# Reordering the first mixer of block 2: compression weights ahead of the later queries, more column steps between turning and weighting, and other places for the weight splits

## The chip, the cores and the metric

The kernel runs on one core of a Trainium2 chip. The metric is the device time of one execution in microseconds, median of several executions. Lower is better.

## The reference, cut to what matters

The network has two blocks of two layers over 256 tokens of width 1024. The change touches one mixer, the first of block 2 (nsa_mixer, called the compressed-and-selected attention below). All in float32:

```
proj = h @ w_in
q, kc_t, vc_t, ks, vs, kw, vw, gate = split(proj)     # q: 16 heads of 64; the rest 4 groups of 64
q, kc_t, ks, kw = rope(...)
kcmp = silu(windows(kc_t) @ cmp_w1[0]) @ cmp_w2[0]     # 15 windows of 32 tokens, 2048 -> 256 -> 64
vcmp = silu(windows(vc_t) @ cmp_w1[1]) @ cmp_w2[1]
p_cmp = softmax(q . kcmp);  o_cmp = p_cmp @ vcmp
o_slc = selected attention(q, ks, vs)                  # at 256 tokens every block is selected
o_win = banded attention(q, kw, vw)
return (g0 * o_cmp + g1 * o_slc + g2 * o_win) @ w_out
```

## The kernel before, in words

**Weights.** Every weight matrix is streamed from memory in units of 128 x 2048 floats (1 MB each), in the order in which they are used. A unit passes four stations. The SyncE queue loads it into one of three buffers `raw` (unit u goes to buffer u mod 3; its load is issued when VectorE has done with unit u-3, which stood there before). ScalarE copies it to `w_hi`, rounded to the short form that TensorE multiplies at full speed (`split_to` in the scalar program, line 1113). VectorE takes the difference `w_lo` (`split_to` in the vector program, line 1527) and sets `lo_done`, which both lets TensorE use the unit and frees its `raw` buffer. `w_hi` and `w_lo` have six places. TensorE multiplies every tile three times (`three`, lines 347, 350 and 351: high by high, high by low, low by high).

**One order per engine.** No scheduler is at work. Each engine runs its instructions in the order in which the code writes them, and waits on semaphores where the code says so. `split_to(n)` splits the units up to n-1 at that place of the engine's order; if a unit has not been loaded yet, the engine stands there, with everything that is written behind it.

**The mixer** is stage `nsa`. Its first unit is u0; below, "unit i" is u0+i. Units 0 to 5 are the first projections, unit 6 the selected values, units 7 and 8 the compression weights of the keys (`compress_weights(.., kv=0)`, 16 column steps of three products each), unit 9 the window values, and then, before the change, unit 10 (queries 1), units 11 and 12 (compression weights of the values), unit 13 (queries 2) and unit 14 (queries 3). Units 15 to 18 are the output projection.

The attention is cut into 20 jobs (`nsa_job`). For each job n, TensorE multiplies `scores(n)` (lines 883 to 887); VectorE takes `maxima(n)` (1926, 1927); ScalarE `exponentials(n)` (1379, 1381); VectorE `weights(n)` (1949, 1950, 1953); GpSimd multiplies the second token tile (`second_tile_weights`, line 2191); TensorE turns the result (`transposed(n)`, 901 to 903; 897 for a compressed job); ScalarE and VectorE copy it out of PSUM (`copy_turned(n)`, lines 1391 and 1958); TensorE multiplies it by the values (`weighted(n)`, 921, 922). "Turning" is `transposed`, "weighting" is `weighted`, and the two copies between them are a hand-over. TensorE fills the time of these chains with column steps of the weight units: the dictionaries in calls such as `unit(10, 6, {1: lambda: transposed(2), ...})` say ahead of which step a piece of the attention stands. A step of `unit` or `values` is two times three products, a step of `compress_weights` three.

The compressed keys and values take their own way: `hidden_exp` and `hidden` (lines 1401; 1974 to 1976) form the silu of a compression, `turn_hidden` (936) turns it, `compress` (944, 948) multiplies by the second matrix. The queries pass `take` (1570, 1571), `times_cos` on GpSimd (2182), `rot` on TensorE (839) and `rope` (1894, 1896).

Of the kernel before, what the change touches and what calls it, by code (L numbers as in the profile page):

```python
# [25 lines left out]
NWIN = GROUPS * NCMP  # L26
# [97 lines left out]
def network_kernel(nc, stream, x_in, consts_in, cols_in, p_in, count_in, table_in, out):  # L124
# [12 lines left out]
    with ctx:  # L137
# [201 lines left out]
        def _(pe):  # L339
# [444 lines left out]
            def nsa(s, u0):  # L784
# [192 lines left out]
                def last_of_first(n):  # L977
                    pe.wait_ge(nsa_v.sem, 2)
                    weighted(n)
# [23 lines left out]
                compress_weights(7, 5, 0, {6: lambda: transposed(0), 10: lambda: (weighted(0), scores(2))})  # L1003
                values(9, 4, {0: lambda: transposed(1), 2: lambda: (weighted(1), scores(3))})
                pe.wait_ge(nsa_v.sem, 1)
                unit(10, 6, {1: lambda: transposed(2), 3: lambda: weighted(2), 5: lambda: transposed(3), 7: lambda: weighted(3)})
                pe.wait_ge(hidc_ready.sem, 1)
                compress_weights(11, 5, 1, {4: lambda: rot(5, 6)})
                pe.wait_ge(nsa_v.sem, 2)
                unit(13, 4, {4: turn_hidden})  # L1010
                pe.wait_ge(rope_done.sem, 5)
                unit(14, 6, {0: compress, 2: lambda: rot(6, 4), 5: lambda: scores(4), 6: lambda: scores(5)})
                rot(7, 6)
                for n in (4, 5):
                    transposed(n)
                    pe.wait_ge(*tA_done.due(me))
                    scores(n + 2)
                weighted_cmp(0, 0)
# [9 lines left out]
                for n in (14, 15):  # L1028
                    transposed(n)
                    pe.wait_ge(*tA_done.due(me))  # L1030
                    scores(n + 2)
# [67 lines left out]
        def _(act):  # L1099
# [251 lines left out]
            def nsa(s, u0):  # L1351
# [47 lines left out]
                def hidden_exp(kv):  # L1399
                    act.wait_ge(unit_used.sem, u0 + 9 + 4 * kv)  # L1400
# [24 lines left out]
                split_to(u0 + 10)  # L1425
                values(0, u0 + 7, 6)
                split_to(u0 + 11)
                copy_turned(0)
                split_to(u0 + 12)
                exponentials(2)  # L1430
                copy_turned(1)
                hidden_exp(0)
                exponentials(3)
                act.wait_ge(unit_used.sem, u0 + 9)
                nc.scalar.activation(hid_hi[:, 0:NWIN * 16], at(NSA_WIN + 16 * NWIN, NWIN * 16), ACT.Copy).then_inc(win_hi.sem, 1)
                values(1, u0 + 10, 4)
                split_to(u0 + 13)
                copy_turned(2)
                split_to(u0 + 14)
                copy_turned(3)  # L1440
                split_to(u0 + 16)
                hidden_exp(1)
                hidden_keys()
# [5 lines left out]
                exponentials(6)  # L1449
                exponentials(7)  # L1450
                heads_high(0)
                for n in range(6, NSA_JOBS):
# [7 lines left out]
                    if n in (7, 8):  # L1460
                        split_to(u0 + 12 + n)
# [966 lines left out]
```

## Time and profile before

| | before |
|---|---|
| median of 3 executions | 1750.73 us (1748.95 to 1754.86) |
| profiled execution, its own time | 1749.38 us |
| its span, first to last instruction | 1747.6 us |
| mean granted TensorE clock | 0.988 of 2.4 GHz |
| TensorE busy | 1677.4 us, 96% of the span |

The span is the time from the first to the last instruction of the profiled execution; the 1.8 us beside it are start and end. TensorE is the engine that is hardly ever idle, so the time goes down only where TensorE waits less, and up where it waits more. The mixer lies between 1013 us and 1228 us of the span.

### The profile page before, as it was taken

Reading aid. Unit: us, or ns where it says so; the run is one execution under the profiler, and the core shown is the slowest. Engines: PE = TensorE matmul, PEld = TensorE weight load, DVE = VectorE, ACT = ScalarE, POOL = GpSimd, SP = SyncE. Lnnn points to the kernel's source line nnn. Section 1 sums busy time; section 2 is a strip of 40 time slices with the busy share of each in tenths; the row PEclk is TensorE's granted clock in tenths of the full one; section 3 lists DMA queues with packets and bytes.
Section 4 is the critical chain, followed back from the end, with each engine's and each line's share of the span. In section 5 each row is a group of like instructions: output and inputs, shape, how many; then the busy total and the mean of one; then the engine's idle time right before and its main releaser. Section 6 shows DMA issues by size and latency. Waiting matters only on the chain.

```text
span 1747.6 us, 29361 instructions
## 1 busy us (share of the span) xinstructions
PE 1677.4 (96%) x12278; PEld 1570.9 (90%) x12278; DVE 1072.3 (61%) x1072; ACT 799.5 (46%) x950; POOL 146.7 (8%) x113
## 2 busy tenths in 40 slices
PE   7999999899999999999999999888899999999998
PEld 7999986799999999989999998756899989888997
DVE  7554776375557755577555687644765567556563
ACT  5343558253435533355434555243544465444442
POOL 1000123010001100012000131121000001000000
PEclk9999999999999999999999999898999999999999
DMA  7545451155453554555453443310365534335551
GB/s 295 201 152 208 159 180 72 73 199 212 150 215 146 193 195 166 200 197 187 157 215 147 161 186 128 130 56 25 123 211 177 188 145 184 108 119 185 179 189 48
DMA packets 39633, 282.27 MB, mean 162 GB/s; under 512 B 4417, under 2 KB 4545, under 8 KB 5761
## 3 DMA queue, kind: packets, MB, share of 16 engines
q1 hardware_dynamic: 39168, 279.59, 43.3%
q8 instruction: 63, 1.03, 0.2%
q0 software_dynamic: 384, 1.51, 0.2%
q14 instruction: 18, 0.14, 0.0%
HBM read 280.04 MB, written 1.05 MB: 161 GB/s over the span
## 4 chain that ended last, share of the span: by engine, by line
PE 87%; DVE 5%; ACT 4%; issue 1%; DMA 1%; POOL 1%; POOLq 0%; DVEq 0%; SPq 0%; ACTq 0%
PE ps L347 27%; PE ps L350 27%; PE ps L351 27%; DVE w_lo L1527 1%; DMA raw<-weights 1%; ACT w_hi L1113 1%; PE ps L883 1%; ACT arena L1381 0%; POOL arena L2191 0%; PE ps L876 0%; DVE arena L1763 0%; ACT arena L1379 0%; DVE X L1668 0%; PE ps L747 0%; PE ps L921 0%
## 5 line engine op out<-in xcount | busy, mean ns | idle before, releaser
L347 PE MATMUL ps<-hT_hi,w_hi 128*128 128x256 f32 x2392 | 683.7, 286 | 15.1 <-DVE hT_lo L1539 12.3
L350 PE MATMUL ps<-hT_lo,w_hi 128*128 128x256 f32 x2392 | 678.2, 284 | 0.0
L351 PE MATMUL ps<-hT_hi,w_lo 128*128 128x256 f32 x2392 | 678.1, 283 | 0.0
L1527 DVE TENSOR_TENSOR w_lo<-raw,w_hi 128x2048 fp32r<-128x2048 f32 x264 | 600.4, 2296 | 124.6 <-ACT w_hi L1113 124.6
L1113 ACT ACTIVATE w_hi<-raw 128x2048 fp32r<-128x2048 f32 x264 | 495.8, 1904 | 40.0 <-DMA raw<-weights 39.9
L347 PEld LDWEIGHTS ps<-hT_hi,w_hi 128*128 128x128 f32 x2392 | 460.1, 192 | 19.2 <-DVE w_lo L1527 11.4
L350 PEld LDWEIGHTS ps<-hT_lo,w_hi 128*128 128x128 f32 x2392 | 460.4, 192 | 2.1 <-issue 1.0
L351 PEld LDWEIGHTS ps<-hT_hi,w_lo 128*128 128x128 f32 x2392 | 460.2, 192 | 0.0
L350 PE MATMUL ps<-hid_lo,w_hi 128*128 128x256 f32 x744 | 211.3, 284 | 0.0
L347 PE MATMUL ps<-hid_hi,w_hi 128*128 128x256 f32 x744 | 210.6, 283 | 0.0
L351 PE MATMUL ps<-hid_hi,w_lo 128*128 128x256 f32 x744 | 208.4, 280 | 0.0
L1154 ACT ACTIVATE sil<-sil 128x512 f32<-128x512 f32 x44 | 27.8, 632 | 345.3 <-DVE sil L1570 345.2
L1570 DVE TENSOR_TENSOR sil<-ps,spare 128x512 f32<-128x512 f32 x47 | 32.5, 691 | 221.0 <-PE ps L351 220.8
L351 PEld LDWEIGHTS ps<-hid_hi,w_lo 128*128 128x128 f32 x744 | 142.9, 192 | 0.0
L350 PEld LDWEIGHTS ps<-hid_lo,w_hi 128*128 128x128 f32 x744 | 142.9, 192 | 0.0
L347 PEld LDWEIGHTS ps<-hid_hi,w_hi 128*128 128x128 f32 x744 | 139.9, 188 | 0.0
L347 PE MATMUL ps<-w_hi,hid_hi 128*128 128x512 f32 (+1 forms) x296 | 114.1, 386 | 4.2 <-DVE hid_lo L1627 3.3
L350 PE MATMUL ps<-w_lo,hid_hi 128*128 128x512 f32 (+1 forms) x296 | 113.9, 385 | 0.0
L351 PE MATMUL ps<-w_hi,hid_lo 128*128 128x512 f32 (+1 forms) x296 | 112.0, 378 | 0.0
L2163 POOL TENSOR_TENSOR arena<-arena 128x512 f32<-128x512 f32 x27 | 40.3, 1491 | 822.5 <-ACT arena L1133 465.0
L347 PE MATMUL ps<-w_hi,hT_hi 128*128 128x512 f32 (+1 forms) x280 | 102.9, 368 | 2.7 <-DVE hT_lo L1962 2.6
L350 PE MATMUL ps<-w_lo,hT_hi 128*128 128x512 f32 (+1 forms) x280 | 99.1, 354 | 0.0
(273 smaller groups left out, 1736.0 us busy)
## 6 DMA issues: line engine op xcount, KB each, us to landing
raw<-weights SPq DMA_DIRECT2D x264, 1024.0 KB, 4.8
X<-x SPq DMA_DIRECT2D x2, 512.0 KB, 6.8
out<-X SPq DMA_DIRECT2D x4, 256.0 KB, 2.1
arena<-p POOLq DMA_DIRECT2D x2, 256.0 KB, 5.3
arena<-counts POOLq DMA_DIRECT2D x1, 512.0 KB, 5.7
arena<-nsa_tables POOLq DMA_DIRECT2D x1, 448.0 KB, 6.8
const<-constants SPq DMA_DIRECT2D x1, 427.0 KB, 9.7
cols<-parameters SPq DMA_DIRECT2D x1, 213.5 KB, 2.5
```

The source lines that it names most:

```text
L347: mm = nc.tensor.matmul(dst, a_hi, b_hi, start=start, stop=False, skip_group_check=True)
L350: nc.tensor.matmul(dst, a_hi, b_lo, start=False, stop=False, skip_group_check=True)
L351: return nc.tensor.matmul(dst, a_lo, b_hi, start=False, stop=stop, skip_group_check=True)
L883: nc.tensor.matmul(bank(a, r * 256, 256), q_of(h, P), k_of(br, h, 256), start=r == 0, stop=False, skip_group_check=True)
L1113: nc.scalar.activation(unit_cols(w_hi, u, 0, UNIT), raw[:, r * UNIT:(r + 1) * UNIT], ACT.Copy).then_inc(hi_done.sem, 1)
L1154: nc.scalar.activation(sil[:, 0:512], sil[:, 0:512], ACT.Silu).then_inc(silu_done.sem, 1)
L1527: nc.vector.tensor_tensor(unit_cols(w_lo, u, 0, UNIT), raw[:, r * UNIT:(r + 1) * UNIT], f(unit_cols(w_hi, u, 0, UNIT)), ALU.subtract).then ...
L1570: return nc.vector.tensor_tensor(chunked(dst), chunked(src), by_token(2), ALU.mult)
L2163: step(nc.gpsimd.tensor_tensor(total, total, at(SQUARES + b * 512, 512), ALU.add))
```

## The change

Four things are done in this one stage; no instruction is added or removed.

1. Units 10 and 11 are now the compression weights of the values, and unit 12 is queries 1. TensorE runs `compress_weights(10, 5, 1, ...)` ahead of `unit(12, ...)`.
2. The steps between `transposed(n)` and `weighted(n)` grow: for job 0 from 4 to 8 compression steps, for jobs 1 to 3 likewise, and jobs 4 to 7 are spread over the steps of unit 14.
3. In ScalarE's order the splits stand in other places relative to `values`, `copy_turned` and `exponentials`.
4. In VectorE's order `maxima`, `weights`, `low_windows`, `hidden`, `take` and the splits are interleaved anew, and the splits that stood between jobs 7 and 9 (on both engines) stand ahead of the steady loop.

```diff
@@ -974,9 +974,10 @@
...
-    def last_of_first(n):
-        pe.wait_ge(nsa_v.sem, 2)
-        weighted(n)
+    def next_scores(n):
+        pe.wait_ge(*tA_done.due(me))
+        scores(n)
...
@@ -1000,22 +1001,20 @@
...
     pe.wait_ge(dup_act.sem, 4)
-    compress_weights(7, 5, 0, {6: lambda: transposed(0), 10: lambda: (weighted(0), scores(2))})
-    values(9, 4, {0: lambda: transposed(1), 2: lambda: (weighted(1), scores(3))})
+    compress_weights(7, 5, 0, {5: lambda: transposed(0), 13: lambda: (weighted(0), scores(2))})
+    values(9, 4, {0: lambda: transposed(1), 4: lambda: (weighted(1), scores(3))})
+    pe.wait_ge(hidc_ready.sem, 1)
+    compress_weights(10, 5, 1, {3: lambda: transposed(2), 10: lambda: weighted(2), 12: lambda: transposed(3)})
     pe.wait_ge(nsa_v.sem, 1)
-    unit(10, 6, {1: lambda: transposed(2), 3: lambda: weighted(2), 5: lambda: transposed(3), 7: lambda: weighted(3)})
-    pe.wait_ge(hidc_ready.sem, 1)
-    compress_weights(11, 5, 1, {4: lambda: rot(5, 6)})
+    unit(12, 6, {2: lambda: weighted(3), 6: turn_hidden})
     pe.wait_ge(nsa_v.sem, 2)
-    unit(13, 4, {4: turn_hidden})
+    unit(13, 4, {1: lambda: rot(5, 6), 4: compress})
     pe.wait_ge(rope_done.sem, 5)
-    unit(14, 6, {0: compress, 2: lambda: rot(6, 4), 5: lambda: scores(4), 6: lambda: scores(5)})
+    unit(14, 6, {0: lambda: scores(4), 1: lambda: scores(5), 2: lambda: rot(6, 4), 5: lambda: transposed(4), 6: lambda: next_scores(6),
+                 7: lambda: transposed(5)})
+    next_scores(7)
+    weighted_cmp(0, 0)
     rot(7, 6)
-    for n in (4, 5):
-        transposed(n)
-        pe.wait_ge(*tA_done.due(me))
-        scores(n + 2)
-    weighted_cmp(0, 0)
     steady(6, ((0, 0), (0, 1)))
...
@@ -1027,8 +1026,7 @@
...
         transposed(n)
-        pe.wait_ge(*tA_done.due(me))
-        scores(n + 2)
+        next_scores(n + 2)
     weighted_cmp(2, 0)
...
@@ -1397,7 +1395,7 @@
...
     def hidden_exp(kv):
-        act.wait_ge(unit_used.sem, u0 + 9 + 4 * kv)
+        act.wait_ge(unit_used.sem, u0 + 9 + 3 * kv)
         nc.scalar.activation(HIDC[0:NWIN, kv * CMP_HID:(kv + 1) * CMP_HID], bank(5, 0, CMP_HID)[0:NWIN], ACT.Exp, scale=-1.0).then_inc(hid_exp.sem, 1)
...
@@ -1422,24 +1420,24 @@
...
     exponentials(1)
-    split_to(u0 + 10)
+    split_to(u0 + 12)
     values(0, u0 + 7, 6)
-    split_to(u0 + 11)
+    split_to(u0 + 13)
     copy_turned(0)
-    split_to(u0 + 12)
+    split_to(u0 + 14)
+    act.wait_ge(unit_used.sem, u0 + 9)
+    nc.scalar.activation(hid_hi[:, 0:NWIN * 16], at(NSA_WIN + 16 * NWIN, NWIN * 16), ACT.Copy).then_inc(win_hi.sem, 1)
     exponentials(2)
...
     hidden_exp(0)
+    split_to(u0 + 15)
     exponentials(3)
-    act.wait_ge(unit_used.sem, u0 + 9)
-    nc.scalar.activation(hid_hi[:, 0:NWIN * 16], at(NSA_WIN + 16 * NWIN, NWIN * 16), ACT.Copy).then_inc(win_hi.sem, 1)
     values(1, u0 + 10, 4)
-    split_to(u0 + 13)
     copy_turned(2)
-    split_to(u0 + 14)
+    split_to(u0 + 16)
     copy_turned(3)
-    split_to(u0 + 16)
     hidden_exp(1)
+    split_to(u0 + 17)
     hidden_keys()
...
@@ -1447,8 +1445,9 @@
...
     exponentials(6)
+    heads_high(0)
     exponentials(7)
-    heads_high(0)
+    split_to(u0 + 19)
     for n in range(6, NSA_JOBS):
...
@@ -1457,8 +1456,6 @@
...
             heads_high({9: 1, 15: 2, 19: 3}[n])
-        if n in (7, 8):
-            split_to(u0 + 12 + n)
     split_to(u0 + 21)
...
@@ -2013,54 +2010,55 @@
...
     nc.vector.tensor_copy(at(GATES, 96), bank(6, 256, 96)).then_inc(gates_ready.sem, 1)
+    maxima(0)
     dve.wait_ge(rope_done.sem, 2)
     take(u0 + 6, 7, QS[1])
-    maxima(0)
     maxima(1)
+    weights(0)
     low_windows(0)
     split_to(u0 + 9)
+    weights(1)
     rope(4, 7, at(KT + 512, 512))
-    weights(0)
-    weights(1)
     split_to(u0 + 10)
...
     copy_turned(1)
-    split_to(u0 + 12)
+    low_windows(1)
     weights(2)
     hidden(0)
+    split_to(u0 + 12)
     maxima(3)
-    low_windows(1)
     copy_turned(2)
...
     copy_turned(3)
-    dve.wait_ge(rope_done.sem, 3)
-    take(u0 + 11, 6, QS[0], QSCALE)
     split_to(u0 + 14)
-    rope(5, 6, at(QT + 512, 512))
-    split_to(u0 + 16)
     hidden(1)
     hidden_values()
+    dve.wait_ge(rope_done.sem, 3)
+    take(u0 + 13, 6, QS[0], QSCALE)
+    split_to(u0 + 15)
+    rope(5, 6, at(QT + 512, 512))
+    compressed()
+    split_to(u0 + 16)
+    maxima(4)
+    maxima(5)
     dve.wait_ge(rope_done.sem, 4)
     take(u0 + 14, 4, QS[1], QSCALE)
-    compressed()
+    weights(4)
+    weights(5)
     rope(6, 4, at(QT + 1024, 512))
     split_to(u0 + 17)
-    maxima(4)
-    maxima(5)
+    t_full.due(me, 2)
+    maxima(6)
     dve.wait_ge(rope_done.sem, 5)
     take(u0 + 15, 6, QS[0], QSCALE)
-    weights(4)
-    weights(5)
+    maxima(7)
+    heads_low(0)
+    weights(6)
     rope(7, 6, at(QT + 1536, 512))
-    split_to(u0 + 18)
-    t_full.due(me, 2)
-    maxima(6)
-    maxima(7)
-    weights(6)
-    heads_low(0)
+    split_to(u0 + 19)
     for n in range(6, NSA_JOBS):
...
@@ -2069,8 +2067,6 @@
...
             heads_low({9: 1, 15: 2, 19: 3}[n])
-        if n in (7, 8):
-            split_to(u0 + 12 + n)
     split_to(u0 + 21)
...
@@ -2397,7 +2393,7 @@
...
     w1 = v["nsa_cmp_w1_2"][0]
-    for part in (kc, vc, ks, qs[0], gates, kw, vs, w1[0], vw, qs[1], w1[1], qs[2], qs[3]):
+    for part in (kc, vc, ks, qs[0], gates, kw, vs, w1[0], vw, w1[1], qs[1], qs[2], qs[3]):
         units += as_units(chunks(part))
...
```

`next_scores(n)` is the wait for `copy_turned` on ScalarE and then `scores(n)`.

The following rows show the built programs. First ScalarE of the kernel before, from the exponentials of job 1 (line 1381) to the copy of job 1 (the second row of line 1391). Line 1113 is the split of a unit, 1367 takes the selected values, 1391 is `copy_turned`.

```order
L1381 ACTIVATE arena,stat<-ps,stat 128x256 x2
L1113 ACTIVATE w_hi<-raw 128x2048
L1367 ACTIVATE arena<-ps,stat 128x256 x2
L1113 ACTIVATE w_hi<-raw 128x2048
L1391 ACTIVATE arena<-ps 128x512
L1113 ACTIVATE w_hi<-raw 128x2048
L1379 ACTIVATE arena,stat<-ps,stat 128x128 x2
L1381 ACTIVATE arena,stat<-ps,stat 128x256 x2
L1391 ACTIVATE arena<-ps 128x512
```

The same place of the changed kernel, where the lines of these helpers have lower numbers (1111, 1365, 1389, 1377 and 1379), and, after the mark, the piece from the split ahead of job 3's exponentials to the copy of job 3.

```order
L1379 ACTIVATE arena,stat<-ps,stat 128x256 x2
L1111 ACTIVATE w_hi<-raw 128x2048 x3
L1365 ACTIVATE arena<-ps,stat 128x256 x2
L1111 ACTIVATE w_hi<-raw 128x2048
L1389 ACTIVATE arena<-ps 128x512
...
L1111 ACTIVATE w_hi<-raw 128x2048
L1377 ACTIVATE arena,stat<-ps,stat 128x128 x2
L1379 ACTIVATE arena,stat<-ps,stat 128x256 x2
L1365 ACTIVATE arena<-ps,stat 128x256 x2
L1389 ACTIVATE arena<-ps 128x512
L1111 ACTIVATE w_hi<-raw 128x2048
L1389 ACTIVATE arena<-ps 128x512
```

Ahead of the first copy (job 0) there stood the splits of units 9 and 10; now there stand those of units 9, 10, 11 and 12. The split of unit 14 stands ahead of the exponentials of job 3 and the copy of job 2, and the split of unit 15 ahead of the copy of job 3; before, units 12 and 13 stood at these places (ahead of the copies of jobs 2 and 3).

Next VectorE of the changed kernel, from the copy of job 0 (line 1955, before 1958) to the split that follows job 3's copy. Line 1524 is the split of a unit (before 1527), 1923 a maximum, 1972 and 1973 the end of `hidden(0)`, 1950 the end of `weights(3)`.

```order
L1955 COPY arena<-ps 128x256
L1524 TENSOR_TENSOR w_lo<-raw,w_hi 128x2048
L1923 TENSOR_REDUCE stat<-ps 128x2
...
L1972 RECIPROCAL arena<-arena 60x256
L1973 TENSOR_TENSOR arena<-arena,ps 60x256
L1524 TENSOR_TENSOR w_lo<-raw,w_hi 128x2048
...
L1950 TENSOR_TENSOR arena<-arena,stat 128x256
L1524 TENSOR_TENSOR w_lo<-raw,w_hi 128x2048
L1955 COPY arena<-ps 128x256
L1524 TENSOR_TENSOR w_lo<-raw,w_hi 128x2048
```

The split of unit 11 (the second of these rows of line 1524) has moved behind `hidden(0)`; before, it stood ahead of `weights(2)` and `hidden(0)`. The split of unit 12 (the third) still stands right behind `weights(3)` and ahead of the copy of job 3.

## Rows read from the trace of the kernel before

**Rows 1.** The page: engines over the span, and the chain that ended last.

```profile
PE 1677.4 (96%) x12278; PEld 1570.9 (90%) x12278; DVE 1072.3 (61%) x1072; ACT 799.5 (46%) x950; POOL 146.7 (8%) x113
...
PE 87%; DVE 5%; ACT 4%; issue 1%; DMA 1%; POOL 1%; POOLq 0%; DVEq 0%; SPq 0%; ACTq 0%
```

**Rows 2.** Windows: stretch, its length, each engine's busy time, granted clock, DMA.

```profile
1064.00:1107.40 43.40, 36.23 (x291) 33.01 (x290) 31.76 (x34) 18.99 (x34) 8.04 (x6) 1.00 0.48 180
...
1107.40:1110.80 3.40, 3.40 (x19) 3.40 (x18) 0.52 (x2) 3.37 (x2) 0.00 (x0) 0.50 0.29 120
...
1127.90:1138.10 10.20, 9.13 (x27) 6.45 (x26) 7.03 (x14) 3.22 (x15) 0.41 (x1) 0.50 0.29 103
```

**Rows 3.** Timeline, TensorE at its waits: start, length, instruction, [idle before <-releaser].

```profile
1064.84 0.30 PE L901 MATMUL ps<-const,arena 128*128 128x128 f32 x1 [0.32 <-POOL arena L2191]
...
1068.66 0.66 PE L921 MATMUL ps<-arena 128*64 128x256 f32 x4 [1.54 <-issue]
...
1087.46 0.66 PE L921 MATMUL ps<-arena 128*64 128x256 f32 x4 [2.14 <-ACT arena L1391]
...
1106.29 0.45 PE L936 MATMUL ps<-const,arena 60*128 60x60 f32 x4 [3.16 <-DVE arena L1976]
...
1125.50 1.12 PE L839 MATMUL ps<-sil,arena 128*128 128x512 f32 x2 [0.85 <-DVE sil L1571]
...
1127.53 0.44 PE L897 MATMUL ps<-const,arena 128*128 128x128 f32 x2 [0.90 <-DVE arena L1944]
...
1128.44 1.22 PE L883 MATMUL ps<-arena 64*128 64x256 f32 x2 [0.47 <-ACT arena L1389]
...
1139.12 0.30 PE L901 MATMUL ps<-const,arena 128*128 128x128 f32 x1 [1.14 <-POOL arena L2191]
```

**Rows 4.** Timeline, TensorE: the first products of two following column steps.

```profile
1101.16 0.28 PE L347 MATMUL ps<-hT_hi,w_hi 128*128 128x256 f32 x1
...
1101.53 0.28 PE L347 MATMUL ps<-hT_hi,w_hi 128*128 128x256 f32 x1
```

**Rows 5.** Timeline, ScalarE: units 10, 11, 15; copy of job 0; exponentials of job 3, windows.

```profile
1063.26 1.97 ACT L1113 ACTIVATE w_hi<-raw 128x2048 fp32r<-128x2048 f32 x1
...
1065.72 0.60 ACT L1391 ACTIVATE arena<-ps 128x512 f32<-128x512 f32 x1 [0.49 <-PE ps L903]
...
1066.94 1.91 ACT L1113 ACTIVATE w_hi<-raw 128x2048 fp32r<-128x2048 f32 x1 [0.62 <-DMA raw<-weights]
...
1081.78 0.37 ACT L1379 ACTIVATE arena<-ps,stat 128x128 f32<-128x128 f32 x1 [6.75 <-DVE stat L1927]
...
1083.38 1.01 ACT L1435 ACTIVATE hid_hi<-arena 128x960 fp32r<-128x960 f32 x1
...
1094.76 1.92 ACT L1113 ACTIVATE w_hi<-raw 128x2048 fp32r<-128x2048 f32 x1 [1.72 <-DMA raw<-weights]
```

**Rows 6.** Timeline, VectorE: units 8, 9, 12; copy of job 0; silu, first and last.

```profile
1059.44 2.29 DVE L1527 TENSOR_TENSOR w_lo<-raw,w_hi 128x2048 fp32r<-128x2048 f32 x1
...
1065.10 3.13 DVE L1527 TENSOR_TENSOR w_lo<-raw,w_hi 128x2048 fp32r<-128x2048 f32 x1
...
1068.15 0.41 DVE L1958 COPY arena<-ps 128x256 f32<-128x256 f32 x1
...
1086.95 2.76 DVE L1527 TENSOR_TENSOR w_lo<-raw,w_hi 128x2048 fp32r<-128x2048 f32 x1 [0.28 <-ACT w_hi L1113]
...
1103.73 0.28 DVE L1974 TENSOR_SCALAR arena<-arena 60x256 f32<-60x256 f32 x1
...
1105.82 0.41 DVE L1976 TENSOR_TENSOR arena<-arena,ps 60x256 f32<-60x256 f32 x1
```

**Rows 7.** Timeline, GpSimd: the multiplications of jobs 0 and 1.

```profile
1063.42 2.66 POOL L2191 TENSOR_TENSOR arena<-arena,stat 128x512 f32<-128x512 f32 x2 [5.47 <-DVE stat L1950]
```

**Rows 8.** Timeline, TensorE: waits in the steady loop.

```profile
1153.01 0.66 PE L921 MATMUL ps<-arena 128*64 128x256 f32 x4 [1.35 <-issue]
...
1159.82 0.66 PE L921 MATMUL ps<-arena 128*64 128x256 f32 x4 [2.04 <-issue]
```

## The prediction

> **What bounds the kernel now.** The page first: TensorE is busy for 96% of the span and holds 87% of the chain that ended last [rows 1]. So the time moves only with TensorE's waits and with its clock. The windows come next: in the mixer TensorE is busy for 36.2 us of 43.4 us between 1064.0 and 1107.4 us, and there are stretches at half clock, 3.4 us from 1107.4 and 10.2 us from 1127.9, each behind waits [rows 2]. The timeline of TensorE then gives every wait that the change could touch: 0.32 and 1.54 us ahead of the turning and weighting of job 0, 2.14 us ahead of the weighting of job 2, 3.16 us ahead of `turn_hidden`, 0.85, 0.90 and twice 0.47 us around jobs 4 to 7 (one row stands for two), 1.14 us ahead of the turning of job 6 [rows 3], and in the steady loop among others 1.35 and 2.04 us [rows 8].
>
> Next, who is late. Behind job 0 it is not ScalarE, whose copy starts at 1065.72 us [rows 5], but VectorE's copy, which starts at 1068.15 us: it stands behind a split of 3.13 us [rows 6], lengthened because GpSimd multiplies jobs 0 and 1 from 1063.42 to 1066.08 us [rows 7]. The reader should take from this that a hand-over waits for every split written ahead of it. The other fact is how far splits can run ahead. VectorE ends unit 8 at 1059.44 + 2.29 = 1061.73 us [rows 6], and ScalarE starts unit 11, in the same raw buffer, at 1066.94 us, released by its transfer [rows 5]: 5.2 us. Unit 12 ends at 1086.95 + 2.76 = 1089.71 [rows 6] and unit 15 starts at 1094.76 us [rows 5]: 5.05 us. So **a unit reaches ScalarE 5.1 us after VectorE has split the unit three before it**, and takes 1.9 us there.
>
> **What the change does, wait by wait.** I walk the new orders of all four engines forward with the durations of the rows. A column step of three products takes 0.36 us [rows 4]. All products stay; TensorE's work costs nothing more.
>
> A. *Weighting of job 0.* ScalarE now has units 9 to 12 ahead of this copy, where it had 9 and 10. Unit 12 needs VectorE to be through with unit 9. That ended at 1065.10 + 3.13 = 1068.2 us [rows 6]; in the new order it ends near 1067.3, because GpSimd's multiplications fall earlier. Unit 12 lands at 1067.3 + 5.1 = 1072.4, is split at 1074.3, and the copy (0.6 us [rows 5]) ends at 1074.9. TensorE began the compression at 1064.84 - 0.32 - 6 x 0.36 = 1062.4, and turns job 0 at 1064.2 without a wait. In the old order the turning and four steps took 1068.66 - 1.54 - 1064.84 = 2.3 us [rows 3]; four more steps make 3.7, so it arrives at 1067.9 us. Wait 7.0 us, where there were 0.32 + 1.54: **+5.1**. Behind it on TensorE stand the scores of job 2, on which VectorE and then ScalarE wait; behind the split on ScalarE stand the copies of jobs 0 and 1.
>
> B. *Weighting of job 2.* Unit 14 now stands ahead of the exponentials of job 3, `values(1)` and the copy of job 2. It needs VectorE's unit 11, which has moved behind `hidden(0)`. The weighting and the scores of job 2 take 0.8 + 1.8 us (1068.66 to 1071.3 in the old order [rows 3]), three steps 1.1, so the first compression ends near 1078.6 us; ScalarE's window copy (1.0), exponentials (1.6, the distance of two rows), copy and exponential of the silu end at 1082.1; `hidden(0)` takes 2.5 us (1103.73 to 1106.23 in the second silu), and unit 11 is done at 1082.1 + 2.5 + 2.3 = 1086.9 [rows 5, 6]. Then 5.1 us of transfer, 1.9 of split, 1.6 of exponentials, 0.6 of values and 0.6 of copy: 1096.7 us. TensorE has 16 + 10 steps (9.4 us), two turnings (1.3) and the weighting and scores of jobs 1 and 3 (2.6) behind 1078.6: it arrives at 1091.9. Wait 4.8 for 2.14 [rows 3]: **+2.7**.
>
> C. *Weighting of job 3.* Unit 15 stands ahead of this copy. It needs unit 12 of VectorE, which stands behind `weights(3)`, so behind the late exponentials: it starts at 1096.3 and ends at 1099.8 (2.2 us, and 1.3 us behind GpSimd's multiplication of job 3, as in [rows 6, 7]). Transfer, split and copy end at 1099.8 + 5.1 + 1.9 + 0.6 = 1107.4 us; TensorE arrives at 1101.7. Wait 5.7 where there was none: **+5.7**.
>
> D. *`turn_hidden`.* Between the second compression and it there now lie six double steps of unit 12 and the wait C. Its silu ends about 1110.3 us (exponential behind the copy of job 3, then 2.5 us), TensorE comes at 1112.5: the 3.16 us go [rows 3]: **-3.2**.
>
> E. *Jobs 4 to 7 and the turning of job 6.* Spread over the steps of unit 14, the short waits of job 4 and 5 vanish, and one of 1.3 us stays ahead of `rot(7)`. The rows have 0.85 + 0.90 + 0.47 + 0.47 + 1.14 us [rows 3], but part of this stretch ran at half clock, where products are longer and waits shorter [rows 2]. Walked at full clock, the old order waits 7.0 us here and the new one 3.9 (2.6 of it ahead of job 6): **-3.1**.
>
> F. *Steady loop.* The splits no longer stand between jobs 7 and 9, where waits of 1.35 and 2.04 us were [rows 8]; they stand ahead of the copy of job 6, whose weighting then waits 3.3 us. **-0.7**. Behind job 9 the two orders are the same.
>
> Sum: 5.1 + 2.7 + 5.7 - 3.2 - 3.1 - 0.7 = **+6.5 us**. The edits in the order of the stream cost nothing, since unit 10 stays a load of the same size.
>
> G. *Clock.* At half clock 3.4 us of busy TensorE do the work of 1.7 us. A wait of 3.16 us was followed by such a stretch, waits of 1.54 and 2.14 us were not [rows 2, 3]. Three waits of 5 to 7 us should each be followed by one: at most 3 x 1.7 = +5.1, at least 0 where the next wait takes the loss in (B and C end on chains that TensorE hardly moves), and the old stretch at 1107.4 (-1.7) may go. I take **+2.5**, between -1.7 and +5.1, nearer the upper end since the new waits are longer than the one that was followed by a stretch.
>
> Total +9.0 us. The profiled execution took 1749.4 us (its span plus 1.8), so 1758.4; the median shown is 1.4 us above it, so 1759.8 or, rounded, **1760 us**, 0.5% slower. What a measurement of this kernel tells from no change is about 0.3%, 5.3 us. The walk has its own error: led over the old order it ends 3 us early over 200 us, its waits within 1 us each. Landing 4.8 us (the page's median) instead of 5.1 takes 0.3 us from A, B and C each.
>
> On waiting in order, the Trainium skill (page TensorE: Matmul & The Clock Gate, section "Architectural detail: the array is 16× 32×32, not 1× 128×128") says that ScalarE and VectorE work strictly first in, first out. The trace agrees, with VectorE's copy at 1068.15 us. Without that rule A, B and C would vanish and the sum be about 1742.
>
> **The rivals.**
> *Faster: the hand-overs are not held.* If unit 12 were in its buffer when ScalarE came to it, the longer distances would do their work: A -1.9, B -2.1, C 0, D -3.2, E and F up to -3.8: 1750.7 less 7 to 11, 1740 to 1744 us. It decides at one point: VectorE must end unit 9 before about 1060 us, and the rows have it at 1068.2 [rows 6]. Chance 0.05.
> *No change.* The waits are as long as I say at A, but B and C are chained to VectorE's unit 11: if the silu and the split end 3 us sooner, or transfers land in 4 us, B and C shrink by 2 to 3 us each and the sum is +2 to +5: 1752 to 1755 us. For it speaks that units 13 to 15 have slack in the old order; against it, the two measured landings. Chance 0.08.
> *More half clock.* Every long wait brings a slow stretch, A's is extended by short waits behind it, as from 1127.9 us where three such lengths followed each other [rows 2], and none is absorbed: 6.5 + 7 and more: 1763 to 1767 us. Chance 0.12, inside "slower".
> The Trainium skill (page TensorE: Matmul & The Clock Gate, section "What's actually happening") calls half rate the default that only activity releases. By that rule alone G would be near +5 and the time 1762 us; the waits of 1.54 and 2.14 us without a stretch behind them speak for less.
> *My forecast:* slower by 5.3 to 12 us, chance 0.75.
>
> **Numbers.** Faster 0.05, same 0.08, slower 0.87 (0.75 + 0.12). The range 1754 to 1767 us takes in the upper half of "no change" and the clock's bound, and leaves the faster case out.
>
> **What would show it.** Right: TensorE's rows of line 921 with waits of about 7, 5 and 6 us, released by ScalarE's copy; ScalarE's split ahead of each released by the transfer; no wait ahead of the transposes of `turn_hidden`; half-clock stretches behind the long waits. Wrong: ScalarE's units 11 and 12 splitting without waiting for a transfer, or the long waits released by VectorE. The prediction fails most likely in E and F, where I compare two chains of many links, and in G.

## The result

The changed kernel takes 1764.34 us (median of 7 runs, 1760.37 to 1766.91), the kernel before 1750.73 us (now of 7 runs, 1748.70 to 1757.70): ratio 1.0068, 95% interval 1.0049 to 1.0087. That is 0.7% slower, or 13.6 us where 9.0 were forecast. The profiled execution took 1764.34 us.

**The page of the changed kernel** [rows 1]: busy time, and the chain that ended last.

```profile
PE 1686.8 (96%) x12278; PEld 1579.2 (90%) x12278; DVE 1072.6 (61%) x1072; ACT 799.8 (45%) x950; POOL 146.9 (8%) x113
...
PE 87%; DVE 5%; ACT 4%; DMA 2%; issue 1%; POOL 1%; POOLq 0%; SPq 0%; DVEq 0%; ACTq 0%
```

The span grew by 15.0 us. TensorE is busy for 9.4 us more with the same 12278 instructions, and idle for 5.6 us more; the same instructions take longer where the clock is granted at half.

To take the other stages out, every profile below is also read from the first product of the first compression to the first transpose behind the mixer (line 448): I call this the mixer time. It is 1228.24 - 1062.24 = 166.0 us before and 178.7 after: +12.7. The other stages gave the rest of the 15.0 us, 1.85 us of it ahead of the compression, where the two programs are the same; the profiles shown below start the compression anywhere from 1061.7 to 1064.9 us.

**Windows of the changed kernel** [rows 2]: length, busy time of PE, PEld, DVE, ACT and POOL, granted clock, DMA.

```profile
1064.09:1242.78 178.69, 145.62 (x872) 116.99 (x871) 90.26 (x164) 63.63 (x170) 25.94 (x20) 0.88 0.21 77
1074.20:1084.40 10.20, 8.19 (x35) 6.84 (x36) 1.02 (x3) 5.15 (x7) 0.00 (x0) 0.50 0.14 61
1101.60:1105.00 3.40, 3.18 (x16) 2.49 (x17) 2.86 (x1) 0.16 (x1) 0.96 (x2) 0.51 0.00 0
1111.80:1115.20 3.40, 3.40 (x17) 2.71 (x18) 2.44 (x3) 2.12 (x2) 0.00 (x0) 0.51 0.23 94
1121.90:1132.20 10.30, 10.30 (x89) 9.69 (x87) 6.62 (x9) 2.00 (x2) 1.50 (x1) 1.00 0.40 138
1132.20:1139.00 6.80, 6.35 (x23) 4.96 (x23) 4.15 (x11) 0.75 (x2) 1.26 (x1) 0.50 0.24 101
1152.80:1163.00 10.20, 7.77 (x30) 5.60 (x29) 5.53 (x9) 0.20 (x1) 1.28 (x1) 0.50 0.55 206
```

The mean granted clock of the mixer time is 0.88; before it was 0.93. With two later stretches (7.0 and 3.4 us) TensorE spends 44 us at 1.2 GHz where it spent 24. The first stretch is 10.2 us long and begins when TensorE has stood idle for 4.7 us. Those at 1101.6, 1111.8 and 1152.8 us lie at or behind the waits of jobs 2, 3 and 6. The one at 1132.2 us does not: TensorE was busy for all of the 10.3 us ahead of it, at full clock. It was working there on units 13 and 14, with `compress` among them, and from 1128.7 us on the small products of `scores(4)` and `scores(5)` (line 876) as well:

```profile
1131.55 3.02 PE L876 MATMUL ps<-arena 64*128 64x32 f32 x16
```

**Timeline of the changed kernel, TensorE at its waits** [rows 3].

```profile
1076.21 1.13 PE L921 MATMUL ps<-arena 128*64 128x256 f32 x4 [6.71 <-ACT arena L1389]
...
1101.82 1.13 PE L921 MATMUL ps<-arena 128*64 128x256 f32 x4 [4.79 <-ACT arena L1389]
...
1111.79 1.13 PE L921 MATMUL ps<-arena 128*64 128x256 f32 x4 [3.29 <-ACT arena L1389]
...
1117.16 0.46 PE L936 MATMUL ps<-const,arena 60*128 60x60 f32 x4
...
1136.60 2.08 PE L839 MATMUL ps<-sil,arena 128*128 128x512 f32 x2 [0.45 <-DVE sil L1568]
...
1151.30 0.30 PE L901 MATMUL ps<-const,arena 128*128 128x128 f32 x1 [2.29 <-POOL arena L2187]
...
1156.54 1.13 PE L921 MATMUL ps<-arena 128*64 128x256 f32 x4 [2.43 <-issue]
```

The three long waits stand where they were forecast, ahead of the weightings of jobs 0, 2 and 3, released by ScalarE's copy. `turn_hidden` (line 936) has no wait. The row of line 839 is `rot(6)`; ahead of `rot(7)`, at 1147.98 us, there is none.

**Timeline of the changed kernel, ScalarE: units 9 and 10, 11, 12, the copy of job 0; the second windows (line 1429); unit 14, the copy of job 2; unit 15, the copy of job 3** [rows 5].

```profile
1061.01 3.72 ACT L1111 ACTIVATE w_hi<-raw 128x2048 fp32r<-128x2048 f32 x2
1069.43 1.91 ACT L1111 ACTIVATE w_hi<-raw 128x2048 fp32r<-128x2048 f32 x1 [4.70 <-DMA raw<-weights]
...
1073.76 1.91 ACT L1111 ACTIVATE w_hi<-raw 128x2048 fp32r<-128x2048 f32 x1 [1.69 <-DMA raw<-weights]
1075.58 0.58 ACT L1389 ACTIVATE arena<-ps 128x512 f32<-128x512 f32 x1
...
1083.12 1.00 ACT L1429 ACTIVATE hid_hi<-arena 128x960 fp32r<-128x960 f32 x1 [4.93 <-PE ps L351]
...
1097.03 1.91 ACT L1111 ACTIVATE w_hi<-raw 128x2048 fp32r<-128x2048 f32 x1 [10.56 <-DMA raw<-weights]
...
1101.14 0.62 ACT L1389 ACTIVATE arena<-ps 128x512 f32<-128x512 f32 x1
1109.34 1.91 ACT L1111 ACTIVATE w_hi<-raw 128x2048 fp32r<-128x2048 f32 x1 [7.58 <-DMA raw<-weights]
1111.16 0.58 ACT L1389 ACTIVATE arena<-ps 128x512 f32<-128x512 f32 x1
```

**Timeline of the changed kernel, VectorE: units 9, 11 and 12, then units 17 and 18 and the copy of job 6** [rows 6].

```profile
1066.50 2.28 DVE L1524 TENSOR_TENSOR w_lo<-raw,w_hi 128x2048 fp32r<-128x2048 f32 x1
...
1089.84 2.28 DVE L1524 TENSOR_TENSOR w_lo<-raw,w_hi 128x2048 fp32r<-128x2048 f32 x1
...
1101.33 3.13 DVE L1524 TENSOR_TENSOR w_lo<-raw,w_hi 128x2048 fp32r<-128x2048 f32 x1
...
1151.62 4.48 DVE L1524 TENSOR_TENSOR w_lo<-raw,w_hi 128x2048 fp32r<-128x2048 f32 x2
1156.02 0.41 DVE L1955 COPY arena<-ps 128x256 f32<-128x256 f32 x1
```

Read the two timelines together: VectorE ends unit 9 at 1068.78 and ScalarE starts unit 12 at 1073.76; unit 11 ends at 1092.12 and unit 14 starts at 1097.03; unit 12 ends at 1104.46 and unit 15 starts at 1109.34. The distances are 4.98, 4.91 and 4.88 us, and behind each split stands the copy that TensorE waits for. **The chain of the changed kernel** goes the same way: VectorE's split, transfer, ScalarE's split (the row "issue", with which it coincides), copy, weighting.

```profile
1066.58 2.21 DVE w_lo L1524
...
1068.94 4.80 DMA raw<-weights
...
1073.78 1.79 issue
1075.58 0.59 ACT arena L1389
...
1076.21 1.13 PE ps L921 x4
```

### The profile page after: what moved, and what is told of

Same layout as the page of the kernel before. It is cut to its first block, busy times and chain, and to the rows that moved or that the text cites. A ratio compares the mean times of both kernels' runs of the same rounds, so it can differ in the third digit from the quotient of the medians.

```text
span 1762.6 us, 29361 instructions
## 1 busy us (share of the span) xinstructions
PE 1686.8 (96%) x12278; PEld 1579.2 (90%) x12278; DVE 1072.6 (61%) x1072; ACT 799.8 (45%) x950; POOL 146.9 (8%) x113
## 4 chain that ended last, share of the span: by engine, by line
PE 87%; DVE 5%; ACT 4%; DMA 2%; issue 1%; POOL 1%; POOLq 0%; SPq 0%; DVEq 0%; ACTq 0%
PE ps L347 27%; PE ps L350 27%; PE ps L351 27%; DMA raw<-weights 2%; DVE w_lo L1524 1%; PE ps L883 1%; ACT w_hi L1111 1%; PE ps L876 0%; PE ps L448 0%; POOL arena L2187 0%; PE ps L921 0%; DVE arena L1760 0%; ACT arena L1379 0%; PE ps L747 0%; PE ps L839 0%
## 5 line engine op out<-in xcount | busy, mean ns | idle before, releaser
L347 PE MATMUL ps<-hT_hi,w_hi 128*128 128x256 f32 x2392 | 684.8, 286 | 14.3 <-DVE hT_lo L1536 11.5
```

The costliest lines, as they stand in the source:

```text
L347: mm = nc.tensor.matmul(dst, a_hi, b_hi, start=start, stop=False, skip_group_check=True)
```

## The experiments

Each kernel's median stands beside runs of the kernel before on the same chip. Mixer time and the mean granted clock of the mixer come from one profile each, and one profile can lie some us off its kernel's median; the ratio is what tells kernels apart.

| kernel | us | before | ratio (95%) | mixer time | clock |
|---|---|---|---|---|---|
| changed kernel | 1764.3 | 1750.7 | 1.0068 (1.0049-1.0087) | 178.7 | 0.88 |
| e1_scalar_back | 1747.0 | 1751.6 | 0.9966 (0.9954-0.9978) | 162.2 | 0.92 |
| e2_scalar_early | 1769.0 | 1751.6 | 1.0098 (1.0085-1.0111) | 185.7 | 0.85 |
| e3_first_place | 1752.8 | 1751.6 | 1.0005 (0.9996-1.0014) | 169.0 | 0.90 |
| e4_later_places | 1756.9 | 1751.6 | 1.0029 (1.0017-1.0041) | 172.2 | 0.88 |
| e5_vector_unit11 | 1759.8 | 1751.4 | 1.0046 (1.0030-1.0061) | 175.2 | 0.87 |
| e6_filled | 1763.3 | 1751.4 | 1.0059 (1.0044-1.0073) | 175.6 | 0.91 |
| e7_mended | 1742.5 | 1751.4 | 0.9944 (0.9927-0.9962) | 158.6 | 0.92 |
| e8_filled_more | 1757.3 | 1752.9 | 1.0021 (1.0009-1.0034) | 172.7 | 0.94 |
| e9_steady | 1740.7 | 1752.9 | 0.9935 (0.9921-0.9949) | 157.7 | 0.90 |
| e10_mended_filled | 1741.2 | 1752.9 | 0.9938 (0.9924-0.9952) | 155.1 | 0.94 |
| e11_old_order_exp | 1757.4 | 1751.1 | 1.0029 (1.0015-1.0043) | 168.3 | 0.94 |
| e12_all | 1740.9 | 1751.1 | 0.9932 (0.9917-0.9947) | 154.8 | 0.93 |

### Whose splits make the waits

**All of ScalarE's splits put back** in the changed kernel:

```diff
-                split_to(u0 + 12)
+                split_to(u0 + 10)
                 values(0, u0 + 7, 6)
-                split_to(u0 + 13)
+                split_to(u0 + 11)
                 copy_turned(0)
-                split_to(u0 + 14)
+                split_to(u0 + 12)
...
                 hidden_exp(0)
-                split_to(u0 + 15)
                 exponentials(3)
                 values(1, u0 + 10, 4)
+                split_to(u0 + 13)
                 copy_turned(2)
-                split_to(u0 + 16)
+                split_to(u0 + 14)
                 copy_turned(3)
+                split_to(u0 + 16)
                 hidden_exp(1)
-                split_to(u0 + 17)
                 hidden_keys()
```

> The changed kernel with only ScalarE's splits put back to the places between the hand-overs where the kernel before has them; TensorE's, VectorE's and the stream's new order stay. My theory (ScalarE's splits of units 11, 12, 14 and 15 ahead of the copies make the three long waits): the waits ahead of the weightings of jobs 0, 2 and 3 fall from 6.7, 4.8 and 3.3 us to under 1 us each, a wait of about 3 us comes back ahead of turn_hidden, and with the long waits most of the added half-clock time goes: 14 us less than the changed kernel's 1764 at full clock, 1743 to 1750 us, so faster than or level with the kernel before. Rival 1 (the longer distances on TensorE or VectorE's moved splits hold it up): the time stays within 4 us of 1764. Rival 2 (the waits go but half-clock time stays, since it belongs to the new order and not to the waits): 1752 to 1757 us.

**The mirror image:** the same splits moved early in the kernel before, nothing else.

> The kernel before with only ScalarE's splits moved ahead of the hand-overs as in the changed kernel; nothing else moved. My theory: the old, shorter distances on TensorE have less cover, so the waits are longer than in the changed kernel: about 9 us ahead of the weighting of job 0, 3 and 7 us ahead of those of jobs 2 and 3, 3 us ahead of turn_hidden; with the clock 1766 to 1776 us. Rival (the splits are cheap where they stand and the other moves make the loss): within 4 us of 1751.

**Only the first group back** (the first three changed lines of the diff):

> The changed kernel with only the first group of ScalarE's splits (units 9 to 13, around values(0) and the copies of jobs 0 and 1) put back; units 14 and 15 still stand ahead of the exponentials of job 3 and of the copy of job 3. My theory: the wait of 6.7 us ahead of job 0's weighting goes, those ahead of jobs 2 and 3 stay at 5 and 3 to 6 us; 7 us less at full clock and one half-clock stretch less: 1753 to 1759 us. Rival (the early wait is absorbed by the later ones, which end on VectorE's chain and not on TensorE): less than 3 us gained, 1761 to 1765 us.

**Only the later ones** (unit 14 behind the copy of job 2, unit 15 behind that of job 3):

> The changed kernel with only the later splits of ScalarE moved: unit 14 behind the copy of job 2, unit 15 behind the copy of job 3; the first group stays early. My theory: the wait of 6.7 us ahead of job 0's weighting stays, those ahead of the weightings of jobs 2 and 3 go, turn_hidden waits 3 us again: 1753 to 1759 us, and together with the first group's gain this adds up to that of all splits put back, to 3 us. Rival (units 14 and 15 then come too late for TensorE's steps and the wait only changes its place): 1761 to 1766 us, with waits for VectorE's splits ahead of the steps of unit 14.

The times are 1747, 1769, 1753 and 1757 us; 17.3 us come back with ScalarE's splits alone. Timeline of e1_scalar_back, TensorE: the wait of job 2, which alone is left of the three, and that of `turn_hidden`.

```profile
1088.20 0.66 PE L921 MATMUL ps<-arena 128*64 128x256 f32 x4 [1.50 <-ACT arena L1389]
...
1099.97 0.45 PE L936 MATMUL ps<-const,arena 60*128 60x60 f32 x4 [2.63 <-DVE arena L1973]
```

Timeline of e2_scalar_early, TensorE at jobs 0 and 3, where the short distances cover less:

```profile
1075.24 1.13 PE L921 MATMUL ps<-arena 128*64 128x256 f32 x4 [8.43 <-ACT arena L1391]
...
1109.24 1.13 PE L921 MATMUL ps<-arena 128*64 128x256 f32 x4 [5.00 <-ACT arena L1391]
```

The theory holds and both rivals of the first run fall: the new order on TensorE, VectorE and in the stream is itself a gain (e1 is 0.3% faster than the kernel before), and most of the added half-clock time goes with the waits (27 us are left of 44; the kernel before has 24). In e3 the wait of job 0 is gone and 5.49 and 3.46 us stay ahead of jobs 2 and 3; in e4 6.71 us stays, the two later ones are gone and `turn_hidden` waits 2.47 us: each wait follows the splits written ahead of its copy. Two expectations of waits missed: in e1 that of job 2 is 1.5 us, not under 1, and in e2 that of job 3 is 5.0 us, not 7 (job 2 and `turn_hidden` wait 2.80 and 2.71 us there, for 3 and 3). The gains of the first group (11.5 us) and the later ones (7.4) add up to 18.9 against 17.3, as expected within 3 us; by the ratios, which take out the difference between the columns "before", they are 11.0 and 6.8 against 17.9. e3 came out 0.2 us under its range; with its 6.7 us of waiting the 10.2 us of half clock behind it went as well.

### The link at job 2

```diff
                 copy_turned(1)
+                split_to(u0 + 12)
                 low_windows(1)
                 weights(2)
                 hidden(0)
-                split_to(u0 + 12)
```

> The changed kernel with VectorE's split of unit 11 moved back ahead of the second windows, weights(2) and hidden(0); ScalarE's splits stay early. It tests the link in my step B: unit 14 reaches ScalarE 5 us after VectorE's split of unit 11. My theory: that split ends near 1074 instead of 1092 us, unit 14 is in its buffer when ScalarE comes to it, and the wait of 4.8 us ahead of job 2's weighting goes to 1 to 2 us; the waits ahead of jobs 0 and 3 stay at about 6.7 and 3 to 6 us. 4 to 6 us less than 1764: 1757 to 1761 us. Rival (ScalarE is late for another reason, its place behind the exponentials or the windows): the wait stays over 4 us and the time within 3 us of 1764.

It took 1759.8 us. Timeline of e5_vector_unit11, VectorE at unit 11:

```profile
1084.55 2.28 DVE L1524 TENSOR_TENSOR w_lo<-raw,w_hi 128x2048 fp32r<-128x2048 f32 x1
```

ScalarE at unit 14 and the copy of job 2, and TensorE's weightings of jobs 2 and 3:

```profile
1092.05 1.92 ACT L1111 ACTIVATE w_hi<-raw 128x2048 fp32r<-128x2048 f32 x1 [5.77 <-DMA raw<-weights]
...
1096.17 0.63 ACT L1389 ACTIVATE arena<-ps 128x512 f32<-128x512 f32 x1
```

```profile
1096.85 0.66 PE L921 MATMUL ps<-arena 128*64 128x256 f32 x4
...
1106.87 1.13 PE L921 MATMUL ps<-arena 128*64 128x256 f32 x4 [4.74 <-ACT arena L1389]
```

The median is in the expected range, but its ratio's interval overlaps that of the changed kernel, so the gain of 4 us is not shown by the times; the profile shows the link. Two numbers missed. VectorE's split ended at 1086.8 us and not near 1074, because ahead of it stands the copy of job 1, which is late through the wait of job 0; so unit 14 was not in its buffer, and ScalarE still waited for the transfer, which ended 5.2 us behind that split. That is 5 us earlier than in the changed kernel, just enough for TensorE to find the copy done: the wait of job 2 is gone and not 1 to 2 us.

### What the clock takes

```diff
+                def filled(n, dst, count):
+
+                    pe.wait_ge(*{0: (rope_done.sem, 4), 2: (nsa_v.sem, 1), 3: (nsa_v.sem, 2)}[n])
+                    for _ in range(count):
+                        nc.tensor.matmul(dst, lhs(hT_hi, 0, 0), hT_hi[:, 0:TOKENS], start=True, stop=True, skip_group_check=True)
+                    weighted(n)
```

> The changed kernel with TensorE kept busy in its three long waits: ahead of the weightings of jobs 0, 2 and 3 it multiplies a tile of hT_hi with another 50, 34 and 20 times into a bank that is overwritten before it is read (at 0.12 us each 6.0, 4.1 and 2.4 us of work that the result doesn't need). The releases of the waits are those of before. Theory 1 (the idle time of TensorE brings the half clock): the half-clock stretches at 1074.2, 1101.6 and 1111.8 us, 17 us together, go, and so do their 5 to 8 us: 1755 to 1760 us, though TensorE multiplies more. Theory 2 (the half clock comes from something else, such as the pattern of work in this stage): the stretches stay, the fillers run at half rate past the release, and the time is 1764 to 1772 us. What my step G left out is what is measured here.

It took 1763.3 us: between the two. The first two stretches went, but the filler of job 3 was too short for its wait, 2.54 us of it stayed, and a stretch from 1108.4 to 1115.2 us stayed with it. The mixer time fell by 3.1 us, the median by about 1, less than the intervals tell apart. So the fillers were made longer, and two more added at job 6:

> The changed kernel with more of TensorE's waits filled with multiplications that the result doesn't need: 50, 42 and 36 ahead of the weightings of jobs 0, 2 and 3 (6.0, 5.0 and 4.3 us), 15 ahead of the turning and 18 ahead of the weighting of job 6 (1.8 and 2.2 us). It asks what the changed order costs at full clock. If my steps A to F are right in size (+6.5 us at full clock) and the rest of the loss is half-clock time, the stretches at 1074, 1101 to 1115 and 1153 to 1163 us are gone and the time is 1756 to 1760 us. Rival: with TensorE at full clock it only waits longer for the same transfers, and what the clock took is nearly all given back as waiting: 1761 to 1764 us; then the loss beyond 6.5 us is not the clock's but sits in steps E and F.

Timeline of e8_filled_more, TensorE: fillers and what is left of the waits at jobs 0, 2 and 3.

```profile
1067.46 6.14 PE L984 MATMUL ps<-hT_hi 128*128 128x256 f32 x50
...
1074.38 0.66 PE L921 MATMUL ps<-arena 128*64 128x256 f32 x4 [0.78 <-ACT arena L1404]
...
1091.23 5.19 PE L984 MATMUL ps<-hT_hi 128*128 128x256 f32 x42
...
1096.95 0.66 PE L921 MATMUL ps<-arena 128*64 128x256 f32 x4 [0.52 <-ACT arena L1404]
...
1102.07 4.48 PE L984 MATMUL ps<-hT_hi 128*128 128x256 f32 x36
...
1106.96 0.66 PE L921 MATMUL ps<-arena 128*64 128x256 f32 x4 [0.42 <-ACT arena L1404]
```

Windows of e8_filled_more: the mixer time, and the stretch over the three waits.

```profile
1062.21:1234.88 172.67, 155.97 (x1033) 130.11 (x1032) 90.26 (x164) 63.75 (x170) 25.93 (x20) 0.94 0.22 80
1067.80:1107.00 39.20, 37.48 (x308) 35.34 (x306) 18.09 (x21) 17.44 (x32) 2.81 (x3) 1.00 0.35 135
```

1757.3 us, with 161 multiplications more than the changed kernel. The granted clock over the three waits is 1.00, in the mixer 0.94, about that of the kernel before, and the mixer time is 6.7 us above that of before. By the ratio e8 is slower than the kernel before by 3.7 us (1.6 to 6.0). The mixer time fell by 6.0 us against the changed kernel, although the hand-overs still hold TensorE up at all three places: filler and rest make 6.9, 5.7 and 4.9 us, where the waits were 6.7, 4.8 and 3.3. Work that nobody needs made the kernel faster, so at these waits the idle time brings the half clock, not the pattern of work. The Trainium skill (page TensorE: Matmul & The Clock Gate, section "What's actually happening") says that throttled is the default and activity releases it; at the filled waits the two runs agree.

That doesn't cover every stretch. Like the changed kernel at 1132.2 us, e8 has one of 6.8 us, from 1127.7 us, with TensorE busy for all of the 10.7 us ahead of it, and no filler was tried there. Why the clock falls at that place was not tested.

### The version that beats both

On ScalarE, over e1_scalar_back:

```diff
                 copy_turned(3)
-                split_to(u0 + 16)
                 hidden_exp(1)
+                split_to(u0 + 16)
                 hidden_keys()
```

and VectorE's unit 11 as in e5.

> TensorE's and the stream's new order with every split behind the hand-over that it held: ScalarE's splits as in the kernel before, the silu's exponential of the second compression ahead of ScalarE's units 14 and 15, and VectorE's unit 11 back ahead of hidden(0). My theory: over the version with ScalarE's splits put back (1747 us) the wait of 2.6 us ahead of turn_hidden shrinks to under 1 us, and the time is 1741 to 1746 us, faster than the kernel before by 0.3 to 0.6%. Rival (that wait covers another chain, such as the turning of job 6, which then takes it over): within 2 us of 1747.

1742.5 us, 0.56% faster than the kernel before. Against e1 it is 4.6 us by the medians, but the two ratios' intervals overlap, so this further gain is not clear of the scatter; and it is of two edits that were not run apart. Timeline of e7_mended, TensorE: `turn_hidden` has no wait left (2.63 us in e1). Part of it came back: the weighting of job 6 waits 3.02 us, and 1.40 in e1.

```profile
1096.01 0.46 PE L936 MATMUL ps<-const,arena 60*128 60x60 f32 x4
```

**The same edit on ScalarE in the old order of TensorE:**

> The kernel before with one ScalarE instruction moved: the exponential of the second silu ahead of the splits of units 14 and 15, as in the mended version; TensorE's old, short distances stay. It asks whether the mended version's gain needs the new order of TensorE. Theory: it does. In the old order turn_hidden stands only four double steps behind the second compression and waits for a VectorE that splits units 14 and 15 first, so the earlier exponential brings nothing there, and the wait of 3.2 us stays: 1750 to 1755 us against 1751.5. Rival: the gain is ScalarE's alone: the wait ahead of turn_hidden shrinks by 2 us and the time is 1745 to 1749 us.

1757.4 us, slower than the kernel before, outside both ranges. Timeline of e11_old_order_exp, VectorE: units 14 and 15, then `hidden(1)`.

```profile
1104.80 4.49 DVE L1527 TENSOR_TENSOR w_lo<-raw,w_hi 128x2048 fp32r<-128x2048 f32 x2 [3.10 <-ACT w_hi L1113]
1109.21 0.28 DVE L1974 TENSOR_SCALAR arena<-arena 60x256 f32<-60x256 f32 x1
```

ScalarE's splits of the same two units, and TensorE at `turn_hidden`:

```profile
1102.87 3.70 ACT L1113 ACTIVATE w_hi<-raw 128x2048 fp32r<-128x2048 f32 x2
```

```profile
1111.77 0.68 PE L936 MATMUL ps<-const,arena 60*128 60x60 f32 x4 [6.36 <-DVE arena L1976]
```

There VectorE splits units 14 and 15 ahead of `hidden(1)`, and it needs ScalarE's halves of them, which now start at 1102.87 us, once ScalarE's exponential has had its bank from TensorE. The wait grew from 3.16 us [rows 3] to 6.36. In e7 VectorE's `hidden(1)` stands ahead of these two units. So by itself the edit costs time in the old order. That it needs VectorE's new order to pay is read from these rows; VectorE's order and TensorE's were not tried apart.

**Three attempts at job 6**: the split of unit 18 behind the copy of job 6 on both engines and `weights(6)` ahead of the heads (e9), fillers of 15 and 18 (e10), both with fillers of 8 and 18 (e12).

> The mended version with the splits of unit 18 on ScalarE and VectorE moved behind the copy of job 6 as well, and the weights of job 6 ahead of the split of VectorE's heads. It looks at my step F: in the changed order ScalarE's copy of job 6 stands behind the split of unit 18. My theory: the waits of 2.3 us ahead of the turning and of 3.0 us ahead of the weighting of job 6 shrink by 1 to 2 us together: 1740 to 1742 us. Rival (that wait is set by the transfer and split of a unit that TensorE needs anyway, or by VectorE's rotation): within 1 us of the mended version.

> The mended version with TensorE kept busy ahead of the turning (15 multiplications, 1.8 us) and the weighting (18, 2.2 us) of job 6. If the idle time there brings the half-clock stretch at 1135 to 1142 us, it goes, and the time falls by 1 to 3 us to 1739 to 1742 us. Rival: the half clock at 1111 to 1118 and 1135 to 1142 us belongs to the short waits ahead of them or is hidden behind the next wait: within 1 us of the mended version, or slower by what the fillers overrun.

> The mended version with both small edits together: the split of unit 18 behind the copy of job 6, the weights of job 6 ahead of the heads, and TensorE kept busy ahead of the turning (8 multiplications, 1.0 us) and the weighting (18, 2.2 us) of job 6. Each alone gave 1 us or less beyond the mended version's 1742.5. If they work on different waits: 1738 to 1741 us. Rival: both move the same idle time, and the next hand-over takes it: 1741 to 1743 us.

1740.7, 1741.2 and 1740.9 us: all within their forecast ranges, but against e7 the ratios' intervals overlap, so no gain of theirs is shown. In e9 the waits at job 6 shrank to 1.12 us and none, but one of 2.27 us came up ahead of the turning of job 7, where the mended version has none:

```profile
1127.81 0.30 PE L901 MATMUL ps<-const,arena 128*128 128x128 f32 x1 [1.12 <-POOL arena L2189]
1135.31 0.45 PE L901 MATMUL ps<-const,arena 128*128 128x128 f32 x1 [2.27 <-POOL arena L2189]
```

## Why the prediction was right, and which term was off

The sign, the mechanism and the range held; the term that was mis-sized is G. The likeliest case did not come: 13.6 us is outside the 5.3 to 12 us that had a chance of 0.75, and the time fell where the rival "more half clock" (0.12) had put it. The range held because it took that rival in.

**A.** Forecast a wait of 7.0 us (+5.1), measured 6.71 (+4.9). Every link is in the rows: unit 9, 5.0 us, unit 12, copy. VectorE's unit 9 ended 1.5 us later than I said (1068.78 for 1067.3) and TensorE came 1.6 us later (1069.50 for 1067.9), which is the shift of 1.85 us that this profile has ahead of the compression. e3 shows that this place is worth 11.5 us with its clock.

**B.** Forecast 4.8 us (+2.7), measured 4.79 (+2.65). The link to unit 11 is shown by e5. That the size fits to the second digit is luck: counted from the start of the compression, TensorE's arrival and the end of the wait both came 3.4 us later than in the walk (32.9 for 29.5 us, 37.7 for 34.3), and the shift fell out of the difference. In e8, without the half clock, this place takes 5.7 us.

**C.** Forecast 5.7 us (+5.7), measured 3.29. The link to unit 12 stands in the rows. The size differs because TensorE was at half clock from 1101.6 to 1105.0 and came later; at full clock, in e8, filler and wait are 4.9 us. There the three places together take 6.9 + 5.7 + 4.9 = 17.5 us, which is what A to C had (7.0 + 4.8 + 5.7). Unit 12 took 3.13 us where the others take 2.28, with GpSimd multiplying job 3 from 1101.03 for 1.28 us. The Trainium skill (page SBUF — State Buffer, section "🔬 SBUF: two separate sides") has the one that comes second blocked for the whole instruction of the other, where VectorE reads two inputs from SBUF and GpSimd reads SBUF too. The trace agrees nearly: 0.98 us of GpSimd's operation were left when the split began, and the split took 0.85 us longer.

**D.** Forecast: the wait of 3.16 us goes. It went.

**E and F.** Forecast -3.1 and -0.7. The waits of jobs 4 and 5 went but for 0.45 us ahead of `rot(6)`; the 1.3 us that I had ahead of `rot(7)` did not come. The wait ahead of the turning of job 6 is 2.29 (I had 2.6), that ahead of its weighting 2.43 (I had 3.3). Summed over the rows shown, the waits from job 4 on were 7.2 us before [rows 3, 8] and are 5.2 us now: 2.0 us less, where the walk at full clock had 3.8. For the weighting of job 6 I blamed the splits on ScalarE and VectorE alike; the rows name VectorE, whose copy of job 6 starts at 1156.02 behind units 17 and 18, while ScalarE's copy ended at 1152.78. The two terms can't be measured apart from the clock. Their sum with A to D can, roughly: e8 has nearly the clock of the kernel before and is 6.7 us behind it in the mixer, where the walk gave +6.5. That is one profile of each; by the ratio it is 3.7 us (1.6 to 6.0), so the near match confirms the size only within some 3 us.

**G.** Forecast +2.5, at most +5.1. Measured: 12.7 - 6.7 = 6.0 us in the mixer; by the ratios of the changed kernel and of e8 0.47%, 8.2 us, give or take 4. The bound took one stretch of 3.4 us for each of three long waits. The wait of 6.71 us brought 10.2 us, the waits at job 6, of 2.29 and 2.43 us, were followed by another 10.2, and 6.8 us from 1132.2 followed no wait at all. I had counted only the new long waits and no stretch longer than the one that the old wait of 3.16 us was followed by, though the kernel before has one of 10.2 us [rows 2]. And I had let B and C absorb it: but ScalarE's second windows wait for the end of TensorE's first compression (the row at 1083.12 us), which fell into the stretch up to 1084.4 us, so B's chain moved with TensorE. Counted from the start of the compression, the weighting of job 2 starts after 37.7 us in the changed kernel and after 34.7 in e8, where that stretch is gone.

Of the rivals, "more half clock" held: 1763 to 1767 us, though one of the stretches behind it came without a wait. The faster one needed VectorE's unit 9 to end before 1060 us, and it ended at 1068.8.

What stays open: how much of the 0.9 us between 12.7 us in the mixer and 13.6 in the medians is other stages' scatter, which of the moves on TensorE, VectorE and in the stream makes e1 faster than the kernel before (they were only run together), and what brings the half clock at 1132.2 us.

## What to carry to other kernels

A split that is written ahead of a hand-over on an engine that works in order can cost the whole chain that frees its buffer: follow it back (here VectorE's split of the unit three before, 5 us of transfer, 1.9 us of split) and write the hand-over first wherever that chain ends later. The new order of the other engines paid only once the hand-overs stood first: 0.7% slower became 0.3% faster with ScalarE's splits put back (e1), and 0.6% with two more moves (e7). And price a wait of TensorE at more than its length: here 14.8 us of waits at three places came with 17 us of half clock, and keeping TensorE busy there and at job 6 took the ratio from 1.0068 to 1.0021.

## What the runs showed of the hardware that was not expected

TensorE got faster through extra work: 161 more multiplications of 0.12 us took the mean granted clock of the mixer from 0.88 to 0.94 (one profile each) and the time from 1.0068 to 1.0021 of the kernel before. A half-clock stretch can also begin within a wait, at 1074.2 us, 2 us ahead of its end, and last 8 us beyond it, with TensorE busy for 8.2 of its 10.2 us. And one can begin with no wait ahead: the stretch of 6.8 us at 1132.2 us, and its likes at 1127.7 us in e8 and 1111.3 us in e7, came when TensorE had been busy without a gap for more than 10 us.
